# A two-layer encoder trunk on one core: the mixer in another order, with single key columns, summed S5 rotation on the tensor engine, and divisions and probability copies on ScalarE

## Time and profile before

| | us |
|---|---|
| median of 3 runs | 1224.56 (1220.88 to 1225.38) |
| the profiled execution | 1224.09 |
| its span on the core | 1222.3 |
| TensorE matmul busy in the span | 1100.7 (90%) |
| VectorE busy | 930.8 (76%) |
| ScalarE busy | 398.7 (33%) |
| GpSimd busy | 70.1 (6%) |
| mixer, first projection to last output matmul, layer 0 | 257.9 to 421.8 |
| the same, layer 1 | 850.1 to 1006.2 |

### The profile page before, as it was taken

How to read it: one execution, slowest core, us unless ns; L and a number is a source line. 1 busy time by engine, 2 the same in 40 slices (tenths; PEclk the granted TensorE clock), 3 DMA queues, 4 the chain that set the end, 5 groups by cost and what they waited for, 6 DMA issues and landing times.

```text
span 1222.3 us, 17280 instructions
## 1 busy us (share of the span) xinstructions
PE 1100.7 (90%) x7041; PEld 954.6 (78%) x7041; DVE 930.8 (76%) x1505; ACT 398.7 (33%) x500; POOL 70.1 (6%) x81
## 2 busy tenths in 40 slices
PE   0799999989959899999979999997996889999995
PEld 0789999867845489999969999996785548999994
DVE  5598899977992579888878997897499457955555
ACT  1345333222131143333334443331122314333341
POOL 1000000012221000000000000000122200000000
PEclk9899999989978889999999999998998898999998
DMA  9698898675220378898866884984243028656630
GB/s 364 216 323 299 285 318 285 202 228 138 70 70 34 121 261 306 287 317 294 311 188 243 291 298 159 320 286 115 69 104 103 1 107 287 218 181 207 206 138 35
DMA packets 197010, 253.19 MB, mean 207 GB/s; under 512 B 41984, under 2 KB 145732, under 8 KB 195908
## 3 DMA queue, kind: packets, MB, share of 16 engines
q1 hardware_dynamic: 196932, 252.09, 61.3%
HBM read 251.03 MB, written 1.05 MB: 206 GB/s over the span
## 4 chain that ended last, share of the span: by engine, by line
PE 73%; DVE 16%; SPq 4%; issue 3%; ACT 2%; POOL 1%; DMA 1%; POOLq 0%; DVEq 0%; ACTq 0%
PE PS L484 13%; PE PS L485 13%; PE PS L486 13%; PE PS L509 6%; PE PS L512 6%; PE PS L513 6%; PE PS L583 6%; PE PS L744 3%; DVE arena L1213 2%; PE PS L466 2%; DVE xn L982 1%; DVE stats L994 1%; DVE xn L989 1%; SPq L292 1%; PE PS L590 1%
## 5 line engine op out<-in xcount | busy, mean ns | idle before, releaser
L484 PE MATMUL PS<-u_hi,w_in_hi 128*128 128x256 f32 x1408 | 401.3, 285 | 2.5 <-DVE u_lo L896 2.5
L485 PE MATMUL PS<-u_lo,w_in_hi 128*128 128x256 f32 x1408 | 397.6, 282 | 0.0
L486 PE MATMUL PS<-u_hi,w_in_lo 128*128 128x256 f32 x1408 | 395.4, 281 | 0.0
L484 PEld LDWEIGHTS PS<-u_hi,w_in_hi 128*128 128x128 f32 x1408 | 268.1, 190 | 8.6 <-issue 7.0
L485 PEld LDWEIGHTS PS<-u_lo,w_in_hi 128*128 128x128 f32 x1408 | 268.6, 191 | 3.2 <-issue 1.9
L486 PEld LDWEIGHTS PS<-u_hi,w_in_lo 128*128 128x128 f32 x1408 | 268.4, 191 | 0.0
L945 DVE TENSOR_TENSOR w_in_lo<-w_in_ring,w_in_hi 128x2048 fp32r<-128x2048 f32 x88 | 201.5, 2290 | 43.7 <-ACT w_in_hi L1515 43.7
L1515 ACT ACTIVATE w_in_hi<-w_in_ring 128x2048 fp32r<-128x2048 f32 x88 | 167.6, 1909 | 48.1 <-DMA w_in_ring<-in_ffn_w_dram 31.2
L865 DVE SCALAR_TENSOR_TENSOR acc<-arena,cs,acc 128x512 f32<-128x512 f32 x217 | 163.2, 752 | 7.7
L509 PE MATMUL PS<-w_out_hi,h_parts 128*128 128x512 f32 x352 | 142.6, 405 | 6.1 <-DVE h_parts L939 6.1
L1523 ACT ACTIVATE w_out_hi<-w_out_ring 128x1024 fp32r<-128x1024 f32 x88 | 88.4, 1053 | 164.4 <-PE PS L513 164.4
(11 more groups left out here) (281 smaller groups left out, 1057.3 us busy)
## 6 DMA issues: line engine op xcount, KB each, us to landing
w_in_ring<-in_ffn_w_dram SPq DMA_DIRECT2D x88, 1024.0 KB, 7.7
arena<-in_ada_w_dram SPq DMA_DIRECT2D x31, 2048.0 KB, 8.2
w_out_ring<-in_ffn_w_dram SPq DMA_DIRECT2D x44, 1024.0 KB, 6.6
w_in_ring<-in_w_in_dram SPq DMA_DIRECT2D x8, 1024.0 KB, 5.8
w_out_ring<-in_w_out_dram SPq DMA_DIRECT2D x4, 1024.0 KB, 6.7
w_in_ring<-in_w_in_dram SPq DMA_DIRECT2D x2, 2048.0 KB, 9.2
w_out_ring<-in_w_out_dram SPq DMA_DIRECT2D x8, 512.0 KB, 4.4
w_in_ring<-in_w_in_dram SPq DMA_DIRECT2D x14, 256.0 KB, 5.1
```

Of the source, the lines that this page charges most:

```text
L484: pe.matmul(y, hi, u_hi[:, kt, :], start=(i == 0), stop=False)
L485: pe.matmul(y, hi, u_lo[:, kt, :], start=False, stop=False)
L486: mm = pe.matmul(y, lo[:, kt, half, :], u_hi[:, kt, :], start=False, stop=(i == KT - 1))
```

## The change

Only the mixer and its two borders change. The feed-forward chunks keep their instructions.

- **Columns.** Index key, sparse key and window keys are loaded once. Index key and sparse key are one product of 96 rows (`kk`), the window keys another (`ka`); ScalarE copies them to the partitions where the heads want them. The gate columns stand beside the token columns (`TOKW` = 204) and are turned by four transposes. 20 products instead of 24, in the order `Z_ORDER`, through banks 4 and 5 only.
- **Order.** TensorE and VectorE lists are rewritten: all four rotations in before the index sums; gate rows, carry and rotations out later; the S5 output in two halves after the mLSTM weights; D's output last.
- **S5 rotation out.** The two sums of products are not formed; TensorE contracts the four products with C (32 matmuls instead of 16). GpSimd's eight additions go.
- **ScalarE** divides the probabilities (`over_sums`), copies all turned ones (`copy_probs`), and does the convolution's lag 0 and half of the GELU's scaling. VectorE's mLSTM norm takes the denominator in at the end.
- **Output.** `w_out` tiles 0 to 3 arrive as two loads in `w_out_ring`; tiles 4 to 7 in the free slot of `w_in_ring` (`last_out`), and their 16 matmuls go bank by bank.
- **Modulation** block 10 (layer 0) moves from the mixer into the last feed-forward chunk, in two halves. Small S5 steps move to chunks 4, 5 and 9. The split of the next weights' second tile moves between the two halves of the norm.

```diff
-NZ = 24
+Z_ORDER = ("ud0", "cq", "ud1", "qi", "qb0", "kk", "t0", "qb1", "t1", "ka", "qa0", "qk0", "qk1", "qk2", "qk3", "qa1",
+           "oc0", "oc1", "v0", "v1")
-ADA = {(0, 0): dict(zip(range(10), range(0, 10))), (0, 1): dict(zip(range(10), range(12, 22))),
+ADA = {(0, 0): dict(zip(range(11), range(0, 11))), (0, 1): dict(zip(range(10), range(12, 22))),
...
# SyncE
                 for m in range(2):
                     load_mix_in(m)
+                if l == 0:
+                    sp.wait_ge(sem("y_ready"), 4)
+                    load_ada(ada_w_2, 11, "ada_2_loaded")
                 for m in range(2):
                     load_mix_out(m)
...
+                for m in range(2, 5):
                     load_mix_in(m)
+                load_last_out()
...
# TensorE
+                def s5_outputs(b):
+                    pe.wait_ge(sem("rotated_out"), l * 4 + (b + 1))
+                    for k in range(2):
+                        i = 2 * b + k
+                        q, t = i % 4, i // 4
+                        parts = ((0, tmp[2 * (b % 2)][:, k * T:(k + 1) * T]), (0, tmp[2 * (b % 2) + 1][:, k * T:(k + 1) * T]),
+                                 (1, st_re[:, i, :]), (1, st_im[:, i, :]))
+                        for p, (ri, moving) in enumerate(parts):
+                            mm = pe.matmul(PS[32 * q:32 * q + 32, 7, t * T:(t + 1) * T], cT[:, ri, t, 32 * q:32 * q + 32],
+                                           moving, start=(p == 0), stop=(p == 3))
+                    mm.then_inc(sem("yd_ready"), 1)
...
+                z_feature("ud0", 0, 0)
+                z_feature("cq", 0, 256)
+                s5_inputs(0)
+                s5_inputs(1)
+                z_feature("ud1", 0, 128)
+                z_low_rank("qi", iq_sb[:, :])
+                spread_gate(l * 3 + 1, 0)
+                s5_inputs(2)
+                z_low_rank("qb0", uq_sb[:, 0:P])
+                s5_inputs(3)
+                z_feature("kk", 0, 384, 96)
+                z_token("t0", 1, 0, TOKW, 0)
...
+                pe.wait_ge(sem("rows_ready"), l * 2 + 2)
...
+                z_feature("oc1", 3, 2 * P)
+                pe.wait_ge(sem("sb_read"), l + 1)
+                scores(lambda h: qaT[:, h // 2, :], lambda h: kaT[:, h // 2, :], half, "sa_ready")
+                pe.wait_ge(sem("pb_ready"), l * 2 + 1)
+                turn_probs(work[0], 0, 6, "ptb_turned")
...
+                y_chunk(0)
+                pe.wait_ge(sem("pc_ready"), l + 1)
+                s5_outputs(0)
+                s5_outputs(1)
+                for b, bank in enumerate((6, 4, 5)):
+                    pe.wait_ge(sem("pa_ready"), l * 2 + 1 + min(b, 1))
+                    turn_probs(work[2], b, bank, "pta_turned")
+                pe.wait_ge(sem("pta_ready"), l * 3 + 3)
...
+                s5_outputs(2)
+                s5_outputs(3)
+                y_chunk(1)
...
                 for b in range(4):
+                    for k in range(4):
+                        if b == 0 and k == 2:
+                            pe.wait_ge(sem("od_ready"), l * 2 + 2)
+                        mm = pe.matmul(PS[:, b, :], oT[:, LAST_TILES + k, tt * P:(tt + 1) * P],
+                                       last_out[:, k, hf * 512:(hf + 1) * 512], start=False, stop=(k == 3))
                     mm.then_inc(sem("y_ready"), 1)
# VectorE, last feed-forward chunk
-                s5_inverse()
-                ffn_tile(0, tile)
-                s5_gains()
...
+                for ft in range(2):
+                    if l == 0:
+                        ada_block(10, ada_w_sb, "ada_loaded", 11, acc_2, ts=range(4 * ft, 4 * ft + 4))
+                    ffn_tile(ft, tile)
+                b_blocks()
# VectorE, mixer
+                gate_diag(1, l * 3 + 1, (2, 6)[l], 0)
+                for k in range(4):
+                    residual(l, 0, k)
+                if l == 0:
+                    ada_block(11, ada_w_2, "ada_2_loaded", 1, summed=10)
                 s5_rotate_in(0)
                 s5_rotate_in(1)
+                gate_diag(1, l * 3 + 1, (2, 6)[l], 1)
+                s5_rotate_in(2)
+                s5_rotate_in(3)
+                for b in range(3):
+                    s5_scan(b, 0)
...
+                s5_rotate_out(2)
+                s5_skip(0)
+                s5_rotate_out(3)
...
-                deepnorm(l, 1)
+                deepnorm(l, 1, lambda: w_in_low(G_FFN2 % 2, 1, ff_tile(l, 1, 0) + 1))
# ScalarE
+                def over_sums(p, ri, ready, signal):
+                    a.wait_ge(sem(ready), l + 1)
+                    for tt, cols in ((0, slice(0, P)), (1, slice(P, 384))):
+                        for h in range(H):
+                            ins = a.activation(p[:, h, cols], p[:, h, cols], ACT.Copy, scale=heads(ri)[:, tt, h:h + 1])
+                        ins.then_inc(sem(signal), 1)
...
+                copy_probs(work[3], 0, 6, "pta_turned", "pta_ready")
+                gelu_square(0)
+                copy_probs(work[3], 1, 4, "pta_turned", "pta_ready")
+                copy_probs(work[3], 2, 5, "pta_turned", "pta_ready")
...
# GpSimd
-                    g.tensor_tensor(st_re[:, tl, :], t4[0], t4[1], ALU.subtract).then_inc(sem("rotated_out"), 1)
-                    g.tensor_tensor(st_im[:, tl, :], t4[2], t4[3], ALU.add).then_inc(sem("rotated_out"), 1)
-                normalise(work[0], ri_b, "rib_ready", "pb_ready")
-                normalise(work[2], ri_a, "ria_ready", "pa_ready")
```

More of the change, by code:

```diff
@@ L88 @@
 ROT_STEPS = 6 * len(TABLE_STEPS)
-NZ = 24
+Z_ORDER = ("ud0", "cq", "ud1", "qi", "qb0", "kk", "t0", "qb1", "t1", "ka", "qa0", "qk0", "qk1", "qk2", "qk3", "qa1",
+           "oc0", "oc1", "v0", "v1")
+ZN = {name: n for n, name in enumerate(Z_ORDER)}
+NZ = len(Z_ORDER)
+TOKW = 204
 def trunk(nc, x, c, ada_w, ada_b, ln_g, ln_b, ffn_w13, ffn_w2, w_in, w_out, sinks, w_uq, w_iq,
@@ new lines, in _ @@
+                z_feature("qk0", 2, 0)
+                z_feature("qk1", 2, P)
+                pe.wait_ge(sem("idx_read"), l + 1)
+                z_copied("qb0", "qb1", "kk")
+                scores(lambda h: qbT[:, h // 2, :], lambda h: kbT, half, "sb_ready")
+                z_feature("qk2", 2, 2 * P)
+                spread_gate(l * 3 + 1, 1)
+                z_feature("qk3", 2, 3 * P)
+                chunk_done(2)
+                chunk_in(3)
+                z_feature("qa1", 3, 0)
+                z_feature("oc0", 3, P)
@@ L999, in deepnorm @@
                     v.tensor_scalar(var_eps[:, tt:tt + 1], mv[:, tt, 1:2], LN_EPS, None, ALU.add).then_inc(sem("var_ready"), 1)
+                    if tt == 0 and between is not None:
+                        between()
                 neg_mean(1)
@@ new lines, in _ @@
+                lf, bsum, gmx = (work[3][0:H, k, 0:T] for k in (1, 2, 3))
+                v.scalar_tensor_tensor(lf, rows[:, 1, :], 0.0, lf, ALU.min, ALU.subtract).then_inc(sem("lf_step"), 1)
+                v.wait_ge(sem("lf_step"), l * 4 + 1)
+                v.tensor_tensor_scan(bsum, ones[0:H, 0:1].to_broadcast([H, T]), lf, 0.0, ALU.mult, ALU.add
+                                     ).then_inc(sem("lf_step"), 1)
+                v.wait_ge(sem("lf_step"), l * 4 + 2)
+                v.tensor_tensor(rows[:, 2, :], rows[:, 0, :], bsum, ALU.subtract).then_inc(sem("lf_step"), 1)
@@ new lines, in copy_probs @@
+                def copy_probs(dst, b, bank, turned, signal):
+                    a.wait_ge(sem(turned), l * 3 + (b + 1))
+                    a.activation(dst[:, :, :].rearrange("p h n -> p (h n)")[:, b * 512:(b + 1) * 512], PS[:, bank, :], ACT.Copy
+                                 ).then_inc(sem(signal), 1)
+                z_copy("ud0", udT[:, 0, :])
+                z_copy("cq", cqT[:, :])
+                z_copy("ud1", udT[:, 1, :])
+                z_copy("qi", qiT[:, :])
+                copy_gate(l * 3 + 1, 1.0, 0)
```

683 lines of the change are left out of this document (329 added, 354 removed).

## The result

The changed kernel takes 1180.01 us, median of 4 runs (1177.63 to 1182.12); the kernel before took 1224.32 beside it (4 runs, 1220.88 to 1225.38). The ratio is 0.9643, 95% interval 0.9628 to 0.9657: 44 us less, where 56 were forecast. The profiled span went from 1222.3 to 1178.3 us.

A forecast was written before the change was run, and what follows sets the result against it. TensorE bounds the mixers, with VectorE's top-k chain last in one place. Summed terms (-27 and -30 per layer, +6 for block 10) gave -51, a walk through the engine queues -62; the middle, -56 from 1224, gave 1168 us, range 1150 to 1191.

The forecast's parts named there:

- Step 1: Mixer projections: 24 products become 20, -14.1 us per layer, all on the path; gate columns and their transposes +0.5.
- Step 2: S5 output matmuls: twice as many cost +2.0 us per layer if they overlap, +7.0 if one after another.
- Step 3: TensorE's wait at the sliding-window scores: VectorE's top-k starts at 31 to 33 us, wait gone, -11.6 us per layer.
- Step 4: Divisions and copies of probabilities on ScalarE: TensorE's waits of 2.6 and 1.8 us per layer go.
- Step 5: Mixer tail: new TensorE waits of +6 us per layer (bounds 2 and 12); second variance earlier, -1.
- Step 6: GpSimd's eight rotation sums go: VectorE gains a us or two where it has slack, so 0.
- Step 7: TensorE's clock in the mixers: fewer waits return 3.3 us in layer 1 and 6.6 in layer 0.
- Step 8: Layer 0's last feed-forward chunk: block 10's load arrives late, normalisation starts later, +6 us (+2 to +10).
- Rival (a): Engine hand-overs: about ten crossings per layer each 1 us later than assumed, giving 1188 us; chance 16%.
- rival (b): Mixers: TensorE's idle returns elsewhere, only the removed products' gain less added costs remains, giving 1207 us; chance 5%.
- (c): More is won: no new waits, full clock, block 10's load hidden, giving about 1148 us; chance 9%.
- (d): Mixers: many short waits hold TensorE at its lower clock level, up to 1408 us; chance 3%.

The follow-up runs named there:

- the grouping: Changed kernel with only the S5 output matmuls reordered so that queue neighbours use different column groups; 1175.61 us, ratio 0.9615 to the kernel before.

## Why the prediction was right, and where it was not

The direction and the range held (1150 to 1191), and 1180.01 lies at the upper edge of the forecast's own band of 1156 to 1180; 12 us of the 56 did not come. The sum from the rows gave 51. Of its miss of 7 us, 6 lie in the feed-forward, which no step priced; the other 5 us come from taking the middle between this sum and the walk's 62. That the mixers came out within 1 us of their sum is in part luck: two errors cancelled, steps 2 and 5.

- **Step 1 (projections), right.** Feature records kept their price, and 3.4 us per product come out at the end.
- **Step 2 (S5 outputs), mis-sized.** Forecast +2.0 per layer with an upper bound of +7.0; measured 19.3 us in both layers against 4.0, +7.6 per layer. The row was the same operation, but not the same order: two matmuls in a row per column group there, four here. The upper bound was the better value, and even it was passed. By itself this is 11 us. It is also the one sign of being wrong that came: output records twice as dear each.
- **Step 3 (the 11.6 us), right.** Top-k began 33.7 us into the stage in layer 0 and 32.4 in layer 1 (forecast 31 to 33), the logits were read out at 52.9 (52 to 54), the wait is gone.
- **Step 4 (ScalarE), right in sum, wrong in cause.** The waits of 2.6 and 1.8 went, but the division would have been off the path on GpSimd too.
- **Step 5 (tail), too dear.** +6 per layer forecast, 1.7 found in layer 0 and 1.7 + 1.3 in layer 1. With it the idle time was 3.4 and 4.5 us instead of the 8.7 and 8.1 of the sum: 8.9 us less, which hides most of step 2's 11.3 too many. One of the reasons is step 2's mistake itself: the long outputs lay over the chain to the copies, as the grouping showed by its wait of 3.53. The borders won 0.7 instead of 1.
- **Step 6 (GpSimd), price right, trade wrong.** The slow addition of the earlier trace rows (1.50 us) did wait for GpSimd: with GpSimd idle it takes 0.56 us.

```profile
314.42 0.56 DVE L1358 TENSOR_TENSOR sc<-sc,mask_b 128x384 f32<-128x384 f32 x1
```

  That the eight additions cost nothing was the forecast (value 0). Then there was nothing to gain by adding TensorE work in their place, and, in the order chosen, 16 us to lose: the forecast priced both sides and did not draw that line. VectorE's wait for the shared buffers (7.27 us) was not seen.
- **Step 7 (clock), right.** 0.97 and 0.96 where 0.95 or more was asked; layer 0 is where most came back. (The three terms that it adds up for layer 1, 3.3, 1.9 and 1.4, make 6.6 and not 6.3.)
- **Step 8 (block 10), right.** +5.8 for +6, with the wait where it was expected.
- **What no step had:** the feed-forward chunks were taken as unchanged. They grew by 5.9 us in the trace, and the runs with moved buffers put 5.0 and 6.5 us on the addresses.

The ledger of busy and idle time was the better of the two sums: -25.9 and -29.2 for the mixers, together 55.1, against 54.3 measured. In layer 1 TensorE is busy 129.3 us instead of the 122.3 forecast, of which step 2 is 5.6 or more, and idle 4.5 instead of 8.1. The walk's 5 to 6 us more per layer did not exist. With the S5 outputs in the other order and its chain mended the kernel takes 1165.96 us, within 2 us of the forecast of 1168 with the cost of the addresses in it; the chain's mending was no part of the forecast.

Rival (a) gave 1188, rival (b) 1207, (c) 1148: the result lies 8 us below (a) and 12 above the forecast. By the number alone (a) is nearer, but its mechanism did not act: the hand-overs cost less than forecast, not more. (d) did not come: the mean clock of the mixers rose.

## What to carry to other kernels

Price an operation by a row of the same operation in the same order: what stands next to a small-tile matmul in the queue can double it. A sum that comes out can hide two errors of opposite sign; compare its terms. Before work is moved to the engine that bounds the stage, ask what the work costs where it is; if the answer is nothing, leave it there. When a buffer is added, compare a stretch that the edit doesn't touch, and try the new buffer behind all others.

## What the runs showed of the hardware

- Matmuls of 32 output columns in all four column groups: 0.060 us a record with neighbours on different groups (1.93 us for 32), 0.063 to 0.068 with two in a row on one (2.0 for 32 before, 1.09 for 16), 0.143 with four in a row at full clock (4.57 for 32) and 0.17 where the clock was low (5.54 for 32, layer 1).
- Buffers moved by 32 bytes made the feed-forward chunks, which TensorE bounds, 0.5% slower (17.72 to 17.80 us) at an unchanged clock and without any idle time; a move of the weight halves by 64 bytes did not.
- A wait of TensorE of 3.5 us was followed by 11 us at a granted clock of 0.56, and one of 0.85 us was not. The wait alone does not decide it. In the kernel after, behind a wait of 1.72 us, the clock stayed at 1.00 in layer 0 and fell to 0.67 in layer 1; and in layer 0 it fell to 0.60 while TensorE was busy throughout and had waited nowhere longer than 0.3 us since the mixer's first projection. What sets it off there is open. Stretches of the kernel after:

```profile
344.00:348.00 4.00, 4.00 (x29) 3.15 (x28) 3.29 (x9) 2.77 (x14) 0.00 (x0) 0.60 0.99 333
365.50:378.00 12.50, 12.38 (x88) 8.33 (x89) 7.20 (x21) 2.22 (x6) 1.66 (x1) 1.00 0.00 0
928.40:938.70 10.30, 10.30 (x65) 7.04 (x64) 3.92 (x13) 0.60 (x1) 1.65 (x1) 0.67 0.00 0
```
- A VectorE addition of two operands in SBUF, 128x384, took 1.50 us beside an addition of GpSimd and 0.56 with GpSimd idle.
